# ScalarE carries the first block product into the second one's PSUM bank, in the loop of the first network

## The reference, cut to what matters

```python
u = jax.nn.relu(rms_norm(h, mlp_norm_g) @ w_up)     # 256x2048 @ 2048x8192
h = h + (u * u) @ w_down                            # 256x8192 @ 8192x2048
```

## Time and profile before

| what | value |
|---|---|
| median of 3 runs | 2431.13 us (2430.9 to 2433.35) |
| profiled execution, its own time | 2432.78 us |
| its span, first to last instruction | 2431.0 us |
| TensorE busy | 2420.1 us, 100% of the span |
| VectorE busy | 1850.0 us, 76% |
| ScalarE busy | 1380.6 us, 57% |

### The profile page before, as it was taken

The page is one execution under the profiler, slowest core; times in us unless marked ns, Lnnn a source line. Parts: engine busy times, 40 slices in busy tenths (PEclk is TensorE's granted clock), DMA queues, the critical chain, the costliest instruction groups (busy, mean ns, idle before and its releaser), DMA issues.

```text
span 2431.0 us, 35431 instructions
## 1 busy us (share of the span) xinstructions
PE 2420.1 (100%) x13195; PEld 2154.0 (89%) x13195; DVE 1850.0 (76%) x2385; ACT 1380.6 (57%) x1868; POOL 66.9 (3%) x57
## 2 busy tenths in 40 slices
PE   9999999999999999999999999999999999999998
PEld 8888888998888888888888889888889999999997
DVE  7676475578989898986555777666888888888877
ACT  7675554655555656555444555566765555555554
POOL 1022120000000000000000000000000000000000
PEclk9999999999999999999999999999999999999999
DMA  9755656556565656566654437675465555555554
GB/s 330 234 173 156 211 188 208 175 190 225 190 224 189 225 188 226 186 219 218 225 171 141 157 110 243 215 264 198 145 224 198 205 206 204 206 204 205 206 209 156
DMA packets 271604, 488.90 MB, mean 201 GB/s; under 512 B 8017, under 2 KB 71025, under 8 KB 270737
## 3 DMA queue, kind: packets, MB, share of 16 engines
q1 hardware_dynamic: 267328, 470.09, 58.3%
q0 software_dynamic: 3312, 13.92, 1.6%
q10 hardware_dynamic: 864, 3.55, 0.4%
HBM read 485.43 MB, written 2.10 MB: 201 GB/s over the span
## 4 chain that ended last, share of the span: by engine, by line
PE 97%; DVE 1%; DMA 1%; ACT 0%; issue 0%; SPq 0%; DVEq 0%; ACTq 0%
PE ps_a L3178 14%; PE ps_a L3180 14%; PE ps_a L3179 14%; PE ps_a L3232 7%; PE ps_b L3935 6%; PE ps_b L3936 6%; PE ps_b L3937 6%; PE ps_a L3233 3%; PE ps_a L3957 2%; PE ps_a L3956 2%; PE ps_a L3955 2%; PE ps_b L3554 2%; PE ps_b L3556 2%; PE ps_b L3555 2%; PE ps_b L3528 1%; PE ps_b L3530 1%
## 5 line engine op out<-in xcount | busy, mean ns | idle before, releaser
L885 ACT CAST whi<-raw 128x1024 fp32r<-128x1024 f32 (+3 forms) x766 | 781.7, 1030 | 635.9 <-PE ps_a L3180 373.5
L1932 DVE TENSOR_TENSOR wlo<-raw,whi 128x1024 fp32r<-128x1024 f32 (+2 forms) x441 | 529.2, 1208 | 327.2 <-ACT whi L885 325.3
L3178 PE MATMUL ps_a<-whi,xhi 128*128 128x512 f32 (+2 forms) x1292 | 483.7, 374 | 0.0
L3180 PE MATMUL ps_a<-whi,xlo 128*128 128x512 f32 (+2 forms) x1292 | 477.7, 370 | 0.0
L3179 PE MATMUL ps_a<-wlo,xhi 128*128 128x512 f32 (+2 forms) x1292 | 477.7, 370 | 0.0
L3178 PEld LDWEIGHTS ps_a<-whi,xhi 128*128 128x128 f32 x1292 | 244.7, 189 | 34.4 <-issue 4.0
L3180 PEld LDWEIGHTS ps_a<-whi,xlo 128*128 128x128 f32 x1292 | 244.6, 189 | 31.3
L3179 PEld LDWEIGHTS ps_a<-wlo,xhi 128*128 128x128 f32 x1292 | 244.7, 189 | 29.9
L3232 PE MATMUL ps_a<-x2both,whi 128*128 128x512 f32 x728 | 241.2, 382 | 0.4 <-DVE wlo L2467 0.4
L3009 DVE TENSOR_TENSOR wlo<-raw,whi 128x1024 fp32r<-128x1024 f32 x171 | 206.2, 1218 | 14.7 <-ACT whi L885 13.3
L3233 PE MATMUL ps_a<-x2both,wlo 128*128 128x256 f32 x728 | 198.4, 273 | 0.0
(11 more groups left out here) (571 smaller groups left out, 4790.5 us busy)
## 6 DMA issues: line engine op xcount, KB each, us to landing
raw<-in_w_down SPq DMA_DIRECT2D x108, 1024.0 KB, 5.2
raw<-in_w_in SPq DMA_DIRECT2D x100, 1024.0 KB, 5.4
raw<-in_w_up SPq DMA_DIRECT2D x82, 1024.0 KB, 5.4
raw_x<-in_w_up SPq DMA_DIRECT2D x26, 1024.0 KB, 6.4
raw<-in_w_gate SPq DMA_DIRECT2D x26, 1024.0 KB, 6.7
raw_g<-in_w_gate SPq DMA_DIRECT2D x18, 1024.0 KB, 8.4
raw<-in_w_out SPq DMA_DIRECT2D x16, 1024.0 KB, 5.1
raw<-in_w_mix_out SPq DMA_DIRECT2D x16, 1024.0 KB, 5.0
```

The costliest lines, as they stand in the source:

```text
L885: return nc.scalar.copy(o, i)
L1932: return V.tensor_tensor(wlo[:, q % 4, :, 0:cols], raw[:, c % SLOTS, 2 * j:2 * j + 2, 0:cols], whi[:, q % 4, :, 0:cols].bitcast(F32), ALU. ...
L3178: mm(o, x0, m0, start=first and j == 0, stop=False)
L3180: ins = mm(o, x1, m0, start=False, stop=last and j == len(kbs) - 1)
```

## The change

ScalarE gets a copy of bank 4 (f0) into bank 5, `seed`, ahead of everything at n = 5 (so ahead of `up_squared`). f1 no longer overwrites bank 5 but accumulates on the copy, and bank 5 then holds f0 + f1. VectorE's `product_add` of f0 goes, and that of f1 adds both at once. TensorE waits for `seed` before f1 (bank 5 is filled) and before f2 (bank 4 has been read). `seed` waits for f0's matmuls and for all earlier `product_add`s. The counts of `d_add` go from 7 to 6 a trip.

```diff
+        seeded, SEED0 = ld["ident"], 16
         T0 = 4 * MLP_TRIPS
         D_FIRST = 2
-        D_LOOP = D_FIRST + 7 * MLP_TRIPS
+        D_LOOP = D_FIRST + 6 * MLP_TRIPS
...
+            def seed(i=None):
+
+                more = 0 if i is None else i
+                act.wait_ge(pe_half, q_mloop + m_count(MAT["f", 0]) + more * MN)
+                act.wait_ge(d_add, D_FIRST + more * 6)
+                copy(bank(m_bank(1)), bank(m_bank(0))).then_inc(seeded, 1)
...
                 for n in range(MN - 1):
+                    if n == MAT["f", 0] + 4:
+                        seed(i)
...
-            PRODUCT_TO = ((0, 0, 1), (0, 0, 1), (0, 1, -1), (1, 1, 1), (1, 1, -1), (0, 1, 1), (1, 0, 1))
+            PRODUCT_TO = (None, (0, 0, 1), (0, 1, -1), (1, 1, 1), (1, 1, -1), (0, 1, 1), (1, 0, 1))
...
-                dve.wait_ge(d_add, D_FIRST + x + more * 7)
+                dve.wait_ge(d_add, D_FIRST + x - 1 + more * 6)
...
-                adds = {MAT["f", x] + 4: x for x in range(7)}
+                adds = {MAT["f", x] + 4: x for x in range(1, 7)}
...
-                pe.wait_ge(d_add, D_FIRST + max(x - 1, 0) + more * 7)
+                if x in (1, 2):
+                    pe.wait_ge(seeded, SEED0 + 1 + more)
+                else:
+                    pe.wait_ge(d_add, D_FIRST + max(x - 2, 0) + more * 6)
...
-                    fresh = form in ("b11", "b21", "t1")
+                    fresh = form in ("b11", "t1")
```

## The result

| | median | range | runs |
|---|---|---|---|
| before | 2432.85 us | 2430.48 to 2435.94 | 22 |
| changed | 2434.65 us | 2433.74 to 2437.54 | 22 |

The changed kernel takes 1.0012 times as long as the one before, with a 95% interval of 1.0006 to 1.0017, that is 1.5 to 4.1 us more. The forecast was 2.75 us more and 2433.9 us. The loss is real but lies under the 0.2% that I had set as the limit between "the same" and "slower". The profiled execution's span went from 2431.0 to 2433.8 us.

What follows compares the result with a forecast made beforehand. TensorE, busy 2420.1 of 2431.0 us, was taken to wait at f3 for the relu; 2.4 us for 11 trips plus 0.35 for trip 0 made 2.75 us more, median 2433.9 us, range 2431.0 to 2436.8.

Steps and rivals of the forecast that it cites:

- What bounds f3: On TensorE in the hardware loop, f3 starts at the later of d1 + 10.42 and relu + 10.00 us.
- The removed additions: On VectorE, 13 additions of 0.744 us each go, ahead of an idle stretch of 1.43 us; gain 0.
- The copy's time: ScalarE's PSUM-to-PSUM copy of 128 x 512 takes 0.587 us; the instruction behind it starts 0.48 us after it.
- The form of the wait: Copy starts 0.28 us behind d1 in the hardware loop (wait its own instruction), 0.20 in trip 0 (wait on copy).
- The sum: Late f3s: 11 trips x (0.76 - 0.54) = 2.4 us, third trip 0, trip 0 0.35; together 2.75 us.
- Rival 1: ScalarE's copy is hidden, 0.22 us shorter; relu at d1 + 0.54, 0 to 1.5 us more, 2431.2 us; chance 0.18.
- Rival 2: VectorE's removed 0.744 us counts, its row up to n = 7 moves forward: 2427.4 to 2428.8 us; chance 0.05.
- Rival 3: ScalarE's bank-to-bank copy costs more, each 0.1 us adding 1.2 us; 2435.8 us with a 0.744 us copy; chance 0.14.

Runs made afterwards that it cites:

- the wait alone: The kernel before, with ScalarE waiting for f0's matmuls at the place of the copy and copying nothing; 2432.56 us, ratio 1.0002 to the kernel before.

## Why the prediction was right, point by point

- **What bounds f3.** The rule "the later of d1 + 10.42 and relu + 10.00" held in the hardware loop of the changed kernel (10.01), with the copy twice (10.01) and with the copy on VectorE (10.00). Shortening the row as the rule says took the wait away. In trip 0 the second distance is 9.90, and with the sums at n = 9 another bound, at u1, shows, which the rule doesn't have.
- **The removed additions are worth nothing.** VectorE's idle stretch grew to 2.29 us (2.1 was forecast), and the subtraction of n = 5 still starts 3.12 us behind the relu. With the sums at n = 16, where the row is shorter, the kernels with and without these additions have the same trips.
- **The copy's time.** It took 0.570 us against 0.587 taken from the earlier trace rows. The difference is worth nothing: the relu starts 0.48 us behind the copy's start either way, so the two register instructions had no price.
- **The form of the wait.** 0.28 us with the wait as an instruction of its own, in the hardware loop, and in trip 0, where it is on the copy, 526.49 - 526.29 = 0.20 us. This is where the forecast comes from: by 0.20 in every trip it would have been 0.9 us lower.
- **The sum.** 11 x (0.76 - 0.54) = 2.4 and 0.35 for trip 0 were forecast. The traces give 11 trips' worth of 2.4 and 0.27 for trip 0 (0.17 at f3 and 0.10 behind it), and 505.47 - 502.80 = 2.67 us in all. Of trip 0's relu I had taken that f3 comes 10.00 us later; it was 9.90.
- **The rivals.** Rival 1, a hidden copy, fell with the relu at d1 + 0.76. Rival 2, VectorE's time counting, fell with the subtraction of n = 5, which starts no sooner behind the relu, and with the two kernels with the sums at n = 16. Rival 3's mechanism, each 0.1 us of copy going into f3, is real, as the doubled copy shows; its price wasn't met. The Trainium skill says in "ScalarE: Activation LUTs", section "Step-by-step: what each stage is for", that ScalarE writes PSUM faster than SBUF. The trace agrees by 17 ns for 512 columns (0.570 against 0.587 us), too little to help.
- **A reading that was wrong.** The prediction calls the product at 740.73 an accumulating one. It is f3, form `t1`, whose first matmul overwrites its bank (`fresh`). What it was to show is true all the same: f1 in the changed kernel accumulates, and its matmuls start 0.216 us apart (733.90 and 734.12).
- **The limit of 0.2%.** It was too wide. 22 runs of each kernel told a change of 0.12% from none.

The absolute time was forecast from a median of three runs, 2431.13, and 22 runs gave 2432.85 for the kernel before. 2434.65 against 2433.9 comes from that, less what the median shows below the trace's 2.7 us (1.8). The interval of the ratio holds both.

Not settled: why the load that the third trip waits for comes late. It did so in every trace of this study, with a relu at d1 + 1.79. In the kernel before, ScalarE waits 4.25 us for it, against 2.9 to 3.1 us in the other trips:

```profile
600.07 2.94 ACT L885 CAST whi<-raw 128x1024 fp32r<-128x1024 f32 x3 [4.25 <-DMA raw<-in_w_down]
```

No run here tries an earlier load.

## What to carry to other kernels

When TensorE is busy 100% of the time, look for the one place per trip where a start comes late, follow it back to the instruction whose distance to it is the same in every trip, and price a change by what it does to that instruction alone. Work moved from the busier engine (VectorE, 76%) to the idler one (ScalarE, 57%) made the kernel slower, because it left an idle stretch on the one and stood ahead of the critical instruction on the other. What helped was to move four short sums past the subtractions that TensorE was waiting for, with an edit of one number. How far they were moved mattered: at n = 9 the next bound, one half earlier, took nearly half of the gain.

## What the runs showed of the hardware

Where ScalarE's wait is an instruction of its own, ahead of the one that works, the working one starts 0.08 us later (0.28 against 0.20 us from the next half's start). The 0.20 was seen in the `up_copy` at n = 14, in the copy of trip 0 (526.49 - 526.29) and in the relu of trip 0 with the wait alone (526.92 - 526.72). A copy of 128 x 512 from one PSUM bank to another takes 0.570 us on ScalarE and 0.696 us on VectorE, and ScalarE's next instruction starts 0.48 us after the copy did. A second copy that waits for the first one's end starts 0.60 us after it. Matmuls that accumulate on a bank that ScalarE has filled are 0.216 us apart, like all others of 512 columns.
